# A decoder block on one core: GpSimd makes 32 steps of stored weight sums instead of VectorE's 12, and half 0 of the second feed-forward product does five stored octets a pass in seven products

## What is computed

```python
h = _rmsnorm(x, ln1_w[l])
proj = jnp.einsum("bsd,de->bse", h, w_in[l])
gdn_qkv, gdn_z, gdn_a, gdn_b, swa_qkv, gate_a, gate_b = _split_cols(proj)
o_a = _gdn_branch(...)      # gated delta rule, 8 heads, chunks of 64
o_b = _swa_branch(...)      # dilated sliding-window attention, 12 heads
y_a = jnp.einsum("bse,ed->bsd", o_a, w_gdn_proj[l])
y_b = jnp.einsum("bse,ed->bsd", o_b, w_swa_proj[l])
mixed = jax.nn.sigmoid(gate_a) * y_a + jax.nn.sigmoid(gate_b) * y_b
x = x + jnp.einsum("bsd,de->bse", mixed, w_out[l])
h = _rmsnorm(x, ln2_w[l])
u = jax.nn.relu(jnp.einsum("bsd,df->bsf", h, w_ff1[l]))
x = x + jnp.einsum("bsf,fd->bsd", jnp.square(u), w_ff2[l])
```

## Time and profile before

| | us |
|---|---|
| median of three runs | 1511.63 |
| span of the profiled execution (the page gives no other time of it) | 1509.3 |
| TensorE busy | 1501.0 |
| VectorE busy | 1110.1 |
| ScalarE busy | 797.8 |
| GpSimd busy | 94.7 |
| DMA, mean over the span | 206 GB/s |

### The profile page before, as it was taken

The page is one execution under the profiler, slowest core; times in us unless marked ns, Lnnn a source line. Parts: engine busy times, 40 slices in busy tenths (PEclk is TensorE's granted clock), DMA queues, the critical chain, the costliest instruction groups (busy, mean ns, idle before and its releaser), DMA issues.

```text
span 1509.3 us, 19446 instructions
## 1 busy us (share of the span) xinstructions
PE 1501.0 (99%) x7484; PEld 1265.2 (84%) x7484; DVE 1110.1 (74%) x1318; ACT 797.8 (53%) x900; POOL 94.7 (6%) x129
## 2 busy tenths in 40 slices
PE   9999999999999999999999999999999999999999
PEld 7888888888888888888888888888888888888887
DVE  6878756878776877776655566688977566679988
ACT  6554444676654544554444545455545444456654
POOL 5000000000040100100000101100000111110000
PEclk9999999999999999999999999999999999999999
DMA  8578897744545444445755655656566666566873
GB/s 290 201 263 291 306 355 261 242 146 166 169 166 167 140 139 142 140 159 172 250 178 185 195 184 184 189 195 218 176 216 198 196 189 186 185 221 235 301 290 147
DMA packets 150086, 310.74 MB, mean 206 GB/s; under 512 B 7680, under 2 KB 8192, under 8 KB 148224
## 3 DMA queue, kind: packets, MB, share of 16 engines
q1 hardware_dynamic: 148752, 307.65, 61.1%
q10 hardware_dynamic: 1264, 2.13, 0.4%
HBM read 295.09 MB, written 14.68 MB: 205 GB/s over the span
## 4 chain that ended last, share of the span: by engine, by line
PE 92%; DVE 4%; DMA 2%; issue 1%; ACT 1%; SPq 0%; DVEq 0%; ACTq 0%
PE banks L564 42%; PE banks L922 16%; PE banks L990 11%; PE banks L968 9%; PE banks L925 8%; PE banks L580 2%; DVE lo L1474 1%; DMA early_sum<-in_w_ff 1%; DVE lo L2085 1%; PE banks L828 1%; DMA raw<-in_w_ff 1%; PE banks L703 1%; PE banks L676 1%; DVE diag L1493 1%; PE banks L819 1%
## 5 line engine op out<-in xcount | busy, mean ns | idle before, releaser
L1474 DVE TENSOR_TENSOR lo<-raw,hi 128x1024 fp32r<-128x1024 f32 x384 | 473.5, 1238 | 283.8 <-ACT hi L1023 281.4
L1023 ACT ACTIVATE hi<-raw 128x1024 fp32r<-128x1024 f32 x383 | 404.8, 1059 | 436.8 <-PE banks L564 261.0
L564 PE MATMUL banks<-hi,st 128*128 128x512 f32 x1600 | 504.3, 396 | 1.3 <-DVE gates L1818 1.1
L564 PEld LDWEIGHTS banks<-hi,st 128*128 128x128 f32 x1600 | 292.4, 188 | 58.1 <-DVE gates L1818 1.4
L922 PE MATMUL banks<-st,hi 128*128 128x512 f32 x1024 | 321.6, 395 | 0.0
L564 PE MATMUL banks<-lo,st 128*128 128x512 f32 x800 | 312.2, 390 | 0.0
L925 PEld LDWEIGHTS banks<-st,lo 128*128 128x128 f32 x1024 | 192.4, 188 | 45.4
L1424 ACT ACTIVATE hi<-raw 128x1024 fp32r<-128x1024 f32 x136 | 144.2, 1061 | 122.6 <-PE banks L990 88.8
L925 PE MATMUL banks<-st,lo 128*128 128x256 f32 x1024 | 201.2, 278 | 0.0
L2085 DVE TENSOR_TENSOR lo<-raw,hi 128x1024 fp32r<-128x1024 f32 x136 | 165.0, 1221 | 33.5 <-ACT hi L1424 28.2
L564 PEld LDWEIGHTS banks<-lo,st 128*128 128x128 f32 x800 | 150.2, 188 | 32.2
(11 more groups left out here) (296 smaller groups left out, 1632.2 us busy)
## 6 DMA issues: line engine op xcount, KB each, us to landing
raw<-in_w_ff SPq DMA_DIRECT2D x122, 1024.0 KB, 5.2
raw<-in_w_in SPq DMA_DIRECT2D x99, 1024.0 KB, 5.0
raw<-in_w_out SPq DMA_DIRECT2D x16, 1024.0 KB, 5.1
early_sum<-in_w_ff SPq DMA_DIRECT2D x12, 1024.0 KB, 7.2
w_sums<-early_sum SPq DMA_DIRECT2D x12, 1024.0 KB, 9.4
raw<-w_sums SPq DMA_DIRECT2D x12, 1024.0 KB, 5.8
raw<-in_w_gdn_proj SPq DMA_DIRECT2D x8, 1024.0 KB, 5.2
raw<-in_w_swa_proj SPq DMA_DIRECT2D x4, 1024.0 KB, 5.2
```

What stands on the lines that cost most here:

```text
L564: last = pe.matmul(acc[:, t], w[:, k0 + 2 * m + kk, P * t:P * t + P], v[:, (i + more) % PIECES, kk, :], start=m == 0 and kk == 0 and a == ...
L1023: act.activation(hi[:, (i + more) % PIECES], raw[:, i // 2 % RAW, 2 * (i % 2):2 * (i % 2) + 2, :], ACT.Copy)\
L1474: dve.tensor_tensor(lo[:, (i + more) % PIECES], raw[:, i // 2 % RAW, 2 * (i % 2):2 * (i % 2) + 2, :], hi[:, (i + more) % PIECES].bitcast(F ...
```

## The change

GpSimd makes and moves the stored sums. It issues the loads and the stores itself and makes the three subtractions with a semaphore wait between them. There are 32 steps: 20 for half 0, which has now five stored octets (0, 2, 3, 5 and 6) in each of two passes and no local one, and 12 for half 1, whose octets stay as they were. Sixteen steps come at the start (buffers at 108 and 116 KB, which `gdn_qkv` takes later), five in the output projection, six between the token sums of half 0 and five between those of half 1 (buffers at 214 and 196 KB). VectorE's write of `gdn_qkv` waits for the stores of the 16 early steps from its third on; ScalarE waits for the late ones before it writes the activations that lie in the late buffers; SyncE waits for the store before it loads a stored tile. The squares' scratch `x_scr2` and the activations' tiles move. The core of the diff:

```diff
-LOCAL = ((0, 3, 5), (2, 5))
-STORED = ((), (0, 3, 6))
+LOCAL = ((), (2, 5))
+STORED = ((0, 2, 3, 5, 6), (0, 3, 6))
...
-SUM_STEPS = [20, 28, 36, 44, 51, 56, 61, 66, 71, 76, 81, 86]
-STORED_SUMS = 3 * len(SUM_STEPS)
+SUM_STEPS = 2 * len(STORED_OCTETS)
+EARLY_STEPS, MIX_STEPS, FF_STEPS = 16, 5, 6
+LATE_STEPS = EARLY_STEPS + MIX_STEPS + FF_STEPS
...
-        x_scr2 = sb("x_scr2", [P, D], F32, 192)
+        x_scr2 = sb("x_scr2", [P, D], F32, 176)
...
-        early = [sb(f"early_sum{n}", [P, 2, 2 * N], F32, 100 + 8 * n) for n in range(2)]
+        early = [sb(f"early_sum{n}", [P, 2, 2 * N], F32, 108 + 8 * n) for n in range(2)]
+        late = [sb(f"late_sum{n}", [P, 2, 2 * N], F32, (214, 196)[n]) for n in range(2)]
...
                 if o in STORED[half] and which >= 2:
-                    src = w_sums[STORED_OCTETS.index((half, np_, o)), :, 2 * which - 4:2 * which - 2]
+                    n = STORED_OCTETS.index((half, np_, o))
+                    for b in range(2):
+                        sp.wait_ge(ev[f"t_out{b}"], 16 * n + 16)
+                    src = w_sums[n, :, 2 * which - 4:2 * which - 2]
...
-            def sums_in(h): ...
-            def sums_out(h): ...
-            def quad_and_sums(q, w, k, c): ...
...
+            def sum_in(h):
+
+                half, np_, o = STORED_OCTETS[h // 2]
+                k = 32 * half + 4 * o + h % 2
+                if h >= 2:
+                    pool.wait_ge(ev[f"t_out{h % 2}"], 16 * (h // 2))
+                pool.dma_start(summed(h)[:], w_2_v[:, k:k + 3:2, span(2 * N * np_, 2 * N)])\
+                    .then_inc(ev[f"t_in{h % 2}"], 16)
+
+            def sum_make(h):
+
+                b = summed(h)
+                lower, upper = b[:, 1], b[:, 0].rearrange("p (c n) -> p c n", c=2)
+                pool.wait_ge(ev[f"t_in{h % 2}"], 16 * (h // 2) + 16)
+                pool.tensor_tensor(upper, b[:, :, N:2 * N], upper, ALU.subtract).then_inc(ev["sum_made"], 1)
+                pool.wait_ge(ev["sum_made"], 3 * h + 1)
+                pool.tensor_tensor(lower[:, N:2 * N], lower[:, N:2 * N], b[:, 0, 0:N], ALU.subtract)\
+                    .then_inc(ev["sum_made"], 1)
+                pool.wait_ge(ev["sum_made"], 3 * h + 2)
+                pool.tensor_tensor(lower[:, 0:N], lower[:, 0:N], lower[:, N:2 * N], ALU.subtract)\
+                    .then_inc(ev["sum_made"], 1)
+
+            def sum_out(h):
+                pool.wait_ge(ev["sum_made"], 3 * h + 3)
+                pool.dma_start(w_sums[h // 2, :, :, h % 2, :], summed(h)[:].rearrange("p r (c n) -> p (r c) n", c=2))\
+                    .then_inc(ev[f"t_out{h % 2}"], 16)
+
+            pool.wait_ge(ev["x_square"], TT)
+            pool.wait_ge(ev["x_split_lo"], KC)
+            sum_in(0)
+            sum_in(1)
+            for h in range(EARLY_STEPS):
+                sum_make(h)
+                sum_out(h)
+                if h + 2 < EARLY_STEPS:
+                    sum_in(h + 2)
 
             pool.wait_ge(ev["w_pt"], 2 * HS)
...
+            pool.wait_ge(piece_used, 8 * QD + 8 + PIECES)
+            sum_in(EARLY_STEPS)
+            pool.wait_ge(ev["m_mixed"], 4)
+            sum_in(EARLY_STEPS + 1)
+            for h in range(EARLY_STEPS, EARLY_STEPS + MIX_STEPS):
+                sum_make(h)
+                sum_out(h)
+                sum_in(h + 2)
+
+            for half, first, end in ((0, EARLY_STEPS + MIX_STEPS, LATE_STEPS), (1, LATE_STEPS, SUM_STEPS)):
+                if half:
+                    pool.wait_ge(piece_used, piece0(0) + HALF_PIECES[0] + PIECES)
+                    sum_in(first)
+                    sum_in(first + 1)
+                for o in range(OCTETS):
+                    pool.wait_ge(ev["u_made"], 8 * half + o + 1)
+                    if o in SEVENS[half]:
+                        token_sums(half, o)
+                    h = first + o
+                    if h < end:
+                        sum_make(h)
+                        sum_out(h)
+                        if h + 2 < end:
+                            sum_in(h + 2)
...
+            def late_stored(half, g):
+
+                end = SUM_STEPS if half else LATE_STEPS
+                b = (g + 1) % 2
+                return ev[f"t_out{b}"], 16 * ((end + 1 - b) // 2)
...
-            def stored_sums(at): ...
...
-                    if n == 0:
+                    if n == 2:
                         for b in range(2):
-                            dve.wait_ge(ev[f"t_out{b}"], 8 * len(SUM_STEPS))
+                            dve.wait_ge(ev[f"t_out{b}"], 8 * EARLY_STEPS)
```

More of the change, by code:

```diff
@@ L85 @@
 STORED_OCTETS = [(half, np_, o) for half in range(2) for np_ in range(2) for o in STORED[half]]
-SUM_STEPS = [20, 28, 36, 44, 51, 56, 61, 66, 71, 76, 81, 86]
-STORED_SUMS = 3 * len(SUM_STEPS)
+SUM_STEPS = 2 * len(STORED_OCTETS)
+EARLY_STEPS, MIX_STEPS, FF_STEPS = 16, 5, 6
+LATE_STEPS = EARLY_STEPS + MIX_STEPS + FF_STEPS
+HALF_TILES = [2 * sum(4 if o in stored else 2 for o in range(OCTETS)) for stored in STORED]
+MORE_QUADS = (HALF_TILES[0] - 32) // 4
 SUMS = 8
@@ L296, in tile_at @@
         def tile_at(half, np_, o, which):
-            return 4 * (QG1 if half else QG0) + tiles_of(half).index((np_, o, which))
+            return 4 * (QG1 + MORE_QUADS if half else QG0) + tiles_of(half).index((np_, o, which))
         def seven(half, o):
@@ L303, in sums_before @@
             before = 2 * len(LOCAL[0]) * half + len(LOCAL[half]) * np_ + LOCAL[half].index(o)
-            return STORED_SUMS + 4 * before
+            return 4 * before
         def source(half, np_, o, n):
             if o in LOCAL[half] and n >= 3:
-                return t_sums[half][n - 3][:], ev["t_made"], sums_before(half, np_, o) + n - 2
+                return t_sums[n - 3][:], ev["t_made"], sums_before(half, np_, o) + n - 2
             if o in STORED[half]:
@@ L315, in source @@
             return raw[:, t % RAW, k:k + 2, :], landed[t % RAW], 16 * (t // RAW) + 16
-        def sums_now(at, after):
-            return [h for h, step in enumerate(SUM_STEPS) if step + after == at]
         def x1_part(np_, t, j):
@@ L342, in product_tile @@
                 if i < RAW:
-                    sp.wait_ge(lo_ready, 2 * t - 6 + MORE_PIECES * half)
+                    sp.wait_ge(lo_ready, piece0(half) + 2 * i - 6)
                 else:
@@ L503, in _, with summed @@
                 made += 4
+            def summed(h):
+                return (early if h < EARLY_STEPS else late)[h % 2]
+            def sum_in(h):
[29 more added lines that the diff above has]
+                    sum_in(h + 2)
             pool.wait_ge(ev["w_pt"], 2 * HS)
@@ L538, in token_sums @@
                 pool.tensor_tensor(s4, a12, s2, ALU.subtract).then_inc(ev["s_made"], 1)
-            for half in range(2):
-                for o in SEVENS[half]:
-                    token_sums(half, o)
+            pool.wait_ge(piece_used, 8 * QD + 8 + PIECES)
[21 more added lines that the diff above has]
+                            sum_in(h + 2)
         @block.tensor
@@ L1019, in split @@
             def split(q, i, more=0):
-                act.wait_ge(landed[i // 2 % RAW], 16 * (q + i // 8) + 16)
+                act.wait_ge(landed[i // 2 % RAW], 16 * (q + i // 8 + (MORE_QUADS if more else 0)) + 16)
                 act.wait_ge(piece_used, 8 * q + i + 1 + more)
@@ L1408, in parts @@
                     u = us[g % 2]
+                    if g == OCTETS - 2:
+                        act.wait_ge(*late_stored(half, g))
                     act.wait_ge(ev["u_made"], g + 8 * half + 1)
@@ L1632, in _ @@
                     steps = {}
-                ahead(QA + n, 8, steps, more_steps=lambda m, n=n: stored_sums(8 * n + m))
+                ahead(QA + n, 8, steps)
                 a_post(n % 2, n)
             for i in range(3):
-                ahead(QA + 6 + i, 8, more_steps=lambda m, i=i: stored_sums(8 * (QA + 6 + i) + m))
+                ahead(QA + 6 + i, 8)
             dve.wait_ge(ev["a_turned"], 6)
@@ L1810, in _ @@
                 steps = {m: both(*a) for m, a in steps.items() if a}
-                ahead(QB + gi, 8, steps, more_steps=lambda m, gi=gi: stored_sums(8 * (QB + gi) + m))
+                ahead(QB + gi, 8, steps)
             def gate(q, g, which, i):
@@ L2093, in weight_sums @@
                 b12, b22 = raw[:, right % RAW, 0:2, :], raw[:, right % RAW, 2:4, :]
-                t1, t2, t3, t4 = (t[:] for t in t_sums[half])
+                t1, t2, t3, t4 = (t[:] for t in t_sums)
                 def make(dst, a, b, n):
```

69 lines of the change are left out of this document (14 added, 55 removed).

## The result

The changed kernel takes 1546.64 us (median of 4 runs, 1545.13 to 1548.88) against 1511.76 beside it (1511.16 to 1512.26): ratio 1.0233, 95% interval 1.0218 to 1.0247. It is 35 us slower; I had forecast 3.

A forecast was written before the change was run, and what follows sets the result against it. It took TensorE's matmul order as the bound, busy 99% of 1509.3 us. Terms -5.4 + 7 + 1.5 = +3.1 gave 1512.4; with 2.3 us from span to run median, 1514.7 us, range 1510 to 1521.

The forecast's parts named there:

- Matmuls removed, -5.4: Half 0's products: two more seven-product octets in each of two passes remove matmuls from TensorE's path, -5.4 us.
- VectorE's relief, 0: Projections and half 0: early_sum and t_sums operations leave VectorE, worth 0 since TensorE hardly waits for them.
- first feed-forward products, 0: Half 0's first products: GpSimd slips 0.2 to 1 us a group, splits have 6 us in hand, cost 0 (to 4).
- Where that falls in the first stage: Six projection turns: GpSimd bursts every 17.6 us hold VectorE and delay TensorE's transposes of t, +7 us (2 to 20).
- The reduce and the small ones don't: Before each first-stage turn: only five large VectorE operations read SBUF twice, the reduce and small ones do not.
- My upper bound of 20: First stage: the most the six turns could lose to GpSimd's holds, 6 x (4.3 - 0.9) = 20 us.
- The hold lasts the whole instruction: VectorE beside GpSimd, both reading two SBUF operands: VectorE is held for GpSimd's whole instruction, 4.3 us a step.
- Second stage +1.5: TensorE's sum of squares after VectorE's sq_lo: one whole burst counted beyond 2.8 us in hand, +1.5 us (0 to 6).
- Early deadline, 0: VectorE's third gdn_qkv write at 361.43 us: the 16 early steps end at 321, 40 us in hand, 0 added.
- The late rival: Early steps hold VectorE at gdn_qkv if their period is over 20.1 us: 1530 us, chance 0.08.
- Later steps, "output projection 0": Output projection: its five steps end at 822 us, before GpSimd's first token sums at 848.75, cost 0.
- Half 0's weights, "3.1 in hand, of which some 2.0 go": Half 0, two stored octets in a row: late last tile uses 2.0 of ACT's 3.1 us in hand, 0 (to 4).

The follow-up runs named there:

- b7: Changed kernel with the edits of e2, e3, e4 and e5, steps 12 early, 6 mix/output projection, 8 half 0, 6 half 1, doubles re-placed: 1508.55 us, ratio 0.9985.
- b6: Changed kernel with the edits of e2, e3, e4 and e5, steps 12 early, 5 output projection, 9 half 0, 6 half 1: 1513.46 us, ratio 1.0017.
- b2: Changed kernel with the edits of e2, e3, e4 and e5, steps 12 early, 5 output projection, 8 half 0, 7 half 1: 1534.90 us, ratio 1.0156.
- d1: Kernel before, with TensorE also waiting at each of six first-stage turns for two one-operand GpSimd operations, no weight sums on GpSimd: 1562.55 us, ratio 1.0336.
- e6: Changed kernel with each step's 1024-element GpSimd subtraction split into two of 512 elements: 1549.17 us, ratio 1.0245.
- e7: Changed kernel with GpSimd's three subtractions a step replaced by one-operand multiplications by 1.0 of the same sizes: 1521.75 us, ratio 1.0061.
- b3: Changed kernel with the edits of e2, e3, e4 and e5, steps 14 early, 6 mix/output projection, 6 half 0, 6 half 1: 1515.67 us, ratio 1.0028.
- e2: Changed kernel with each early step waiting for a TensorE piece count, at most one step per group, away from the turn: 1531.15 us, ratio 1.0130.
- e5: Changed kernel with the five output projection steps each held for the fourth piece of a group, one per group: 1541.97 us, ratio 1.0201.
- e3: Changed kernel with the products of a pass in the order t1, t3, t2, t4: 1540.49 us, ratio 1.0197.
- e4: Changed kernel with half 1's first group waiting for all but the last three first sums of half 0: 1542.62 us, ratio 1.0212.
- e1: Changed kernel with GpSimd's subtractions left out, loads and stores kept: 1515.63 us, ratio 1.0034.

## Why the prediction was wrong

- **Matmuls removed, -5.4: right.** It is 160.7 against 165.9 us where nothing is late.
- **VectorE's relief, 0; first feed-forward products, 0: right.** Half 0's takes 179.22 us, before 179.21. (The six steps there were free, and so were eight in b7; where they lay badly, they cost 4.2 us in b6 and 6.4 in b2.)
- **"Where that falls in the first stage", +7: this step failed; it was 28.2.** It has four parts. The period was 13.7 and not 17.6 us, mostly because I took the landing of stores from SyncE's crowded queue. I walked the bursts at fixed times against turns at fixed times; but a turn that waits moves, and with 13.7 us a period none came through (that the two settled into step is read from the starts, not tested). "The reduce and the small ones don't" was wrong: a small TENSOR_SCALAR was held 2.1 us, and small two-operand ones about 1 us. That happened at one turn of the six; at the others the large operations that I had named were held. So a hit turn lost 2.4 to 3.8 us, near my bound of 4.3 - 0.9 = 3.4. (The others do not quite have "the same pattern" as the second: the first has 0.3 us in hand and not 0.9.) And I charged a stall at its own length, while TensorE's clock added 1.6 us behind each in the mean (d1). My upper bound of 20 stood for the waits alone, 18.7 measured; the 9.5 behind them I had at nothing.
- **The hold lasts the whole instruction: right** (3.70 us at the fourth turn, some 1.22 of its own and 2.42 of GpSimd's; 2.24 beside 2.48 at the second, half as much in e6). By the Trainium skill (SBUF — State Buffer, Who interferes with whom), VectorE's tensor_scalar contends as well where it runs in a two-port mode; the trace agrees that it can be stopped, with 2.24 against 0.17 us, once, though it does not show the mode, and I had used only the page's rule on two inputs. Its rule that any GpSimd operation reading SBUF stops a two-input VectorE operation went further than e7 did: 1.95 against 1.22 us, beside 2.80 us of GpSimd's.
- **Second stage +1.5: near by luck** (28.2 at its first turn and 28.3 at the output projection: 0), because the faster steps ended at 253 us. With later steps it cost 6 to 12 us (b3, e2), on the convolution, which I had not looked at; my window was sq_lo's.
- **Early deadline, 0: right.** The late rival was excluded by the same faster landing.
- **Later steps, "output projection 0": +4.0.** I compared the end of the steps with the next user of GpSimd and did not ask what the bursts would hold, nor what the transfers would do to w_out's tiles; e5 takes it back.
- **Half 0's weights, "3.1 in hand, of which some 2.0 go": wrong by the size of the first.** ACT may split a piece only when the piece four before is used, which leaves 3 x 1.36 = 4.1 us ahead and not 5.4; less 2.3 for the two copies 1.8 in hand, and with a landing of 7.5 us in place of 6.5 the four passages lost 6.3 us (e3). The 2.0 at the end of half 0, for first sums that now come from a stored octet, I had not seen at all (e4). The time is the sum of these: 28.2 + 4.0 + 3.8 in half 0 (the matmuls' gain taken off) = 36.0 at half 1's first group.

## What to carry to other kernels

A background engine's instruction that holds another engine is priced by the chain it meets, not by its share of time. The 270 us of GpSimd work that the change adds cost some 30 us where the change puts them (e1); in b7, placed anew and with e3's and e4's edits, about 3 of the 5.4 us are lost. Tie such steps to the progress of the engine that bounds, not to their own transfers. And a stall of a saturated TensorE can cost more than its length: look at the granted clock behind it, which fell behind some stalls of 2 to 3 us here and not behind others.

## What the runs showed of the hardware that I had not expected

- Behind five of six stalls of 2.3 to 3.7 us, TensorE's granted clock was 0.50 for 2.7 to 5.7 us of work (1.4 to 2.7 us lost each), behind the sixth, of 3.0 us, not at all; behind stalls of 5.5 to 7.8 us (d1) it was 0.50 for 3.7 to 5.7 us (2.1 lost in the mean).
- VectorE's TENSOR_SCALAR on 128x8, 0.17 us alone, took 2.24 us beside a two-operand GpSimd instruction (once), and up to 1.69 beside one-operand ones and their DMA issues.
- GpSimd reading one operand slowed VectorE's two-operand work by 0.3 to 0.7 us an instruction where two operands stopped it.
- Four convolution operations of 256 elements took 5.63 us instead of 1.13 beside GpSimd's burst, which itself ran at its shortest then (1.28 us for 512 elements, against 2.16 in other bursts).
